# State-space layer of a hybrid backbone: output weights loaded ahead of the last running sums, two state buffers, the variance of y on another engine, one product moved

## What is computed

```python
def step(h, inp):
    xc, ac, Bc, Cc = inp
    acum = jnp.cumsum(ac, axis=1)
    Lm = jnp.exp(jnp.where(tri, acum[:, :, None, :] - acum[:, None, :, :], -jnp.inf))
    CB = jnp.einsum('blgn,bsgn->bgls', Cc, Bc)
    y_diag = jnp.einsum('bgls,blsgr,bsgrp->blgrp', CB, Lm, xg)
    y_off = jnp.einsum('blgn,bgrpn->blgrp', Cc, hg) * jnp.exp(acum)[..., None]
    h_new = jnp.exp(acum[:, -1])[:, :, None, None] * h + jnp.einsum('bsgn,bsgr,bsgrp->bgrpn', Bc, w_end, xg)
    return h_new, y_diag + y_off

def gated_rms_norm(y, z, w):          # groups of 256 columns
    g = y * jax.nn.silu(z)
    return g * lax.rsqrt(jnp.mean(g * g, axis=-1) + EPS) * w
```

## Time and profile before

| | |
|---|---|
| median of 3 executions | 1497.12 us (1496.01 to 1497.76) |
| profiled execution, its own time | 1492.21 us |
| its span, first to last instruction | 1491.0 us |
| PE busy | 1354.5 us (91%) |
| DVE busy | 940.1 us (63%) |
| ACT busy | 773.5 us (52%) |
| POOL busy | 437.3 us (29%) |
| second layer's groups | from about 862 us; the last group's own work 1320 to 1386 us |
| one steady group (groups 1 to 6) to the next | 64.9 us |

### The profile page before, as it was taken

How to read it: one execution, slowest core, us unless ns; L and a number is a source line. 1 busy time by engine, 2 the same in 40 slices (tenths; PEclk the granted TensorE clock), 3 DMA queues, 4 the chain that set the end, 5 groups by cost and what they waited for, 6 DMA issues and landing times.

```text
span 1491.0 us, 22906 instructions
## 1 busy us (share of the span) xinstructions
PE 1354.5 (91%) x8120; PEld 1179.8 (79%) x8120; DVE 940.1 (63%) x1661; ACT 773.5 (52%) x1566; POOL 437.3 (29%) x411
## 2 busy tenths in 40 slices
PE   4999899999999999989997989899999999976797
PEld 4888898899889889868876778887878888765575
DVE  4696656566665666554107668887888888867312
ACT  4432556556555645543217556666666667555331
POOL 0000012112111112113222253544446364435243
PEclk9999999999999999999999999999999999997898
DMA  9344112111112111235412132323222232422531
GB/s 366 110 162 142 43 60 99 56 53 53 62 59 90 53 54 54 74 120 161 147 41 107 43 90 85 98 70 110 87 84 93 76 99 70 112 71 64 211 107 56
DMA packets 46933, 141.31 MB, mean 95 GB/s; under 512 B 5920, under 2 KB 6432, under 8 KB 46880
## 3 DMA queue, kind: packets, MB, share of 16 engines
q1 hardware_dynamic: 42272, 130.12, 26.5%
q10 hardware_dynamic: 4608, 10.49, 2.2%
HBM read 125.78 MB, written 14.81 MB: 94 GB/s over the span
## 4 chain that ended last, share of the span: by engine, by line
PE 48%; DVE 16%; ACT 11%; issue 10%; POOL 8%; DMA 4%; SPq 1%; DVEq 0%; ACTq 0%; POOLq 0%
PE psL L1947 13%; PE psC L1947 6%; PE psS L1932 3%; POOL xw L1909 3%; PE psS L1934 3%; PE psS L1933 3%; ACT X L1016 2%; PE psT L2093 2%; PE psV L1932 2%; PE psV L1934 2%; PE psV L1933 2%; DMA Y1raw<-y_spill 2%; PE psL L1932 2%; PE psL L1934 2%; PE psL L1933 2%
## 5 line engine op out<-in xcount | busy, mean ns | idle before, releaser
L1775 POOL TENSOR_TENSOR wlo<-wraw,whi 128x1024 fp32r<-128x1024 f32 x63 | 150.7, 2393 | 481.9 <-ACT whi L649 402.3
L1947 PE MATMUL psL<-hhi,whi 128*128 128x512 f32 x304 | 123.5, 406 | 0.0
L1947 PE MATMUL psL<-hlo,whi 128*128 128x512 f32 x304 | 122.5, 403 | 0.0
L1947 PE MATMUL psL<-hhi,wlo 128*128 128x512 f32 x304 | 120.6, 397 | 0.0
L2254 PE MATMUL psL<-h1hi,whi 128*128 128x512 f32 x256 | 103.4, 404 | 0.3 <-DVE X L1520 0.3
L2254 PE MATMUL psL<-h1lo,whi 128*128 128x512 f32 x256 | 102.0, 399 | 0.0
L2254 PE MATMUL psL<-h1hi,wlo 128*128 128x512 f32 x256 | 101.9, 398 | 0.0
L1357 DVE TENSOR_REDUCE smax<-psS 128x1 f32<-128x256 f32 (+3 forms) x96 | 67.9, 708 | 51.3 <-PE psS L1934 51.3
L1388 DVE TENSOR_TENSOR PTlo<-psT,PThi 128x256 fp32r<-128x256 f32 (+3 forms) x96 | 68.1, 709 | 48.8 <-ACT PThi L807 47.5
L649 ACT ACTIVATE whi<-wraw 128x1024 fp32r<-128x1024 f32 x54 | 56.6, 1051 | 62.3 <-PE psV L1934 62.3
L1947 PE MATMUL psC<-hhi,whi 128*128 128x256 f32 x280 | 81.9, 292 | 4.9 <-ACT whi L649 2.2
(11 more groups left out here) (423 smaller groups left out, 4486.2 us busy)
## 6 DMA issues: line engine op xcount, KB each, us to landing
wraw<-in_w_ssm SPq DMA_DIRECT2D x48, 512.0 KB, 3.2
wraw<-in_w_in SPq DMA_DIRECT2D x40, 512.0 KB, 3.9
wraw<-in_w_out SPq DMA_DIRECT2D x32, 512.0 KB, 4.1
sums<-sum_spill SPq DMA_DIRECT2D x32, 512.0 KB, 4.8
ada<-in_w_ada SPq DMA_DIRECT2D x16, 512.0 KB, 14.3
wraw<-in_w_ada_late SPq DMA_DIRECT2D x16, 512.0 KB, 4.5
X<-in_xc SPq DMA_DIRECT2D x12, 512.0 KB, 9.6
y_spill<-Yst SPq DMA_DIRECT2D x16, 384.0 KB, 2.5
```

The source lines that it names most:

```text
L1775: G_.tensor_tensor(wlo[:, par], wraw[:, slot], f(whi[:, par]), ALU.subtract).then_inc(s_weight_lo, 1)
L1947: last = PE_.matmul(out, a, b, start=i == 0 and not shared, stop=i == 3 * KT - 1, skip_group_check=True)
```

## The change

1. SP issues the first four loads of output weights before the running sums of chunks 2 and 3 of the last group; before, two came between these and two behind both.
2. `hcur` becomes two buffers. Step i writes buffer i % 2 and reads the other one. DVE's addition in step i waits for the lo part of step i - 2 and not of step i - 1, and only from i = 3.
3. The variance: ACT's square takes a scale, so that its sum is the mean (a quarter of it, as before) at once, and writes its unused squares into `ynm`. POOL adds EPS from a new tile `tiny` ahead of its power. `variance1` on DVE goes, and DVE gets a wait for its own gated tile of the chunk before.
4. PE makes the diagonal product of chunk 0 in state step 4 right behind the state's own product, ahead of two half projections; before it came behind them.

```diff
+    tiny = sbuf(keep, "tiny", [P, 1])
...
-        hcur = sbuf(s, "hcur", [P, DIRS * GW])
+        hcur = sbuf(s, "hcur", [P, 2, DIRS * GW])
...
+        for c in range(NR):
+            out1_load(c)
         sums_load(SSM_GROUPS - 1, 2)
-        for c in range(NR):
-            if c == 2:
-                sums_load(SSM_GROUPS - 1, 3)
-            out1_load(c)
+        sums_load(SSM_GROUPS - 1, 3)
         y1_store(SSM_GROUPS - 1)
...
-            A_.activation(y1[:, 0:GW], yg, ACT.Square, accum_out=yss[:, 0:1]).then_inc(s_y_squares, 1)
+            A_.activation(ynm[:], yg, ACT.Square, scale=(0.25 / GW) ** 0.5, accum_out=yss[:, 0:1]).then_inc(s_y_squares, 1)
...
-                    A_.activation(Hhi[:, i - 1, 0, :], hcur[:, 0:GW], ACT.Copy)
-                    A_.activation(Hhi[:, LT - i, 1, :], hcur[:, GW:2 * GW], ACT.Copy).then_inc(s_state_hi, 1)
+                    A_.activation(Hhi[:, i - 1, 0, :], hcur[:, i % 2, 0:GW], ACT.Copy)
+                    A_.activation(Hhi[:, LT - i, 1, :], hcur[:, i % 2, GW:2 * GW], ACT.Copy).then_inc(s_state_hi, 1)
...
-        def variance1(g, c):
-            dve.wait_ge(s_y_squares, LT * g + c + 1)
-
-            V_.tensor_scalar(yvv[:, 0:1], yss[:, 0:1], 0.25 / GW, EPS, ALU.mult, ALU.add).then_inc(s_y_variance, 1)
-
...
-                    V_.tensor_tensor(by_head(hdec[:], HD), by_head(hcur[:], HD), per_head(GP[:, R_DEC + i], 0, DIRS, HD),
+                    V_.tensor_tensor(by_head(hdec[:], HD), by_head(hcur[:, (i - 1) % 2], HD), per_head(GP[:, R_DEC + i], 0, DIRS, HD),
...
-                    if i > 1:
-                        dve.wait_ge(s_state_lo, LT * g + i - 1)
-                    V_.tensor_tensor(hcur[:], hdec[:], ybank[0], ALU.add).then_inc(s_state_new, 1)
+                    if i > 2:
+                        dve.wait_ge(s_state_lo, LT * g + i - 2)
+                    V_.tensor_tensor(hcur[:, i % 2], hdec[:], ybank[0], ALU.add).then_inc(s_state_new, 1)
...
+                if c:
+                    dve.wait_ge(s_y_gated1, n)
                 dve.wait_ge(s_x_d, n + 1)
                 dve.wait_ge(s_y_chunk, n + 1)
                 V_.tensor_tensor(y2, ybank[1][:, 0:GW], xD[:, c % 2], ALU.add).then_inc(s_y_diag_d, 1)
...
-                variance1(g, c)
...
+        G_.memset(tiny[:], EPS)
...
+                pool.wait_ge(s_y_squares, n + 1)
+                G_.tensor_tensor(yvv[:, 0:1], yss[:, 0:1], tiny[:], ALU.add).then_inc(s_y_variance, 1)
                 pool.wait_ge(s_y_variance, n + 1)
                 inv_sqrt(yrs[:, 0:1], yvv[:, 0:1], 1, s_y_rstd)
...
+            def y_diag(c):
+                n = LT * g + c
+                pe.wait_ge(s_cb_decayed_lo, n + 1)
+                if c:
+                    pe.wait_ge(s_y_diag_d, n)
+                for h in range(GH):
+                    x, m = slice(h * HD, (h + 1) * HD), slice(h * P, (h + 1) * P)
+                    last = mm3(ybank[1][:, h * HD:(h + 1) * HD], Mhi[:, m], Mlo[:, m], xthi[:, c, x],
+                               xtlo[:, c, x], True, True)
+                last.then_inc(s_y_chunk, 1)
...
+                if i == STEPS - 1:
+                    pe.wait_ge(s_tokens_lo, g + 1)
+                    y_diag(0)
                 next_part(i)
                 if last_group and i >= 3:
                     out1_fill(i - 3)
             next_part(STEPS)
-            pe.wait_ge(s_tokens_lo, g + 1)
             for c in range(LT):
                 n = LT * g + c
-                pe.wait_ge(s_cb_decayed_lo, n + 1)
                 if c:
-                    pe.wait_ge(s_y_diag_d, n)
-                for h in range(GH):
-                    x, m = slice(h * HD, (h + 1) * HD), slice(h * P, (h + 1) * P)
-                    last = mm3(ybank[1][:, h * HD:(h + 1) * HD], Mhi[:, m], Mlo[:, m], xthi[:, c, x],
-                               xtlo[:, c, x], True, True)
-                last.then_inc(s_y_chunk, 1)
+                    y_diag(c)
```

More of the change, by code:

```diff
@@ L1665, in ssd @@
                 if i == 0:
-                    V_.tensor_copy(hcur[:], ybank[0]).then_inc(s_state_new, 1)
+                    V_.tensor_copy(hcur[:, 0], ybank[0]).then_inc(s_state_new, 1)
                 else:
-                    if i > 1:
-                        dve.wait_ge(s_state_lo, LT * g + i - 1)
-                    V_.tensor_tensor(hcur[:], hdec[:], ybank[0], ALU.add).then_inc(s_state_new, 1)
+                    if i > 2:
+                        dve.wait_ge(s_state_lo, LT * g + i - 2)
+                    V_.tensor_tensor(hcur[:, i % 2], hdec[:], ybank[0], ALU.add).then_inc(s_state_new, 1)
                 if i + 2 < STEPS:
@@ L1914, in state_lo @@
             pool.wait_ge(s_state_hi, LT * g + i)
-            G_.tensor_tensor(Hlo[:, i - 1, 0, :], hcur[:, 0:GW], f(Hhi[:, i - 1, 0, :]), ALU.subtract)
-            G_.tensor_tensor(Hlo[:, LT - i, 1, :], hcur[:, GW:2 * GW], f(Hhi[:, LT - i, 1, :]),
+            G_.tensor_tensor(Hlo[:, i - 1, 0, :], hcur[:, i % 2, 0:GW], f(Hhi[:, i - 1, 0, :]), ALU.subtract)
+            G_.tensor_tensor(Hlo[:, LT - i, 1, :], hcur[:, i % 2, GW:2 * GW], f(Hhi[:, LT - i, 1, :]),
                              ALU.subtract).then_inc(s_state_lo, 1)
```

## The result

| | median of the executions | ratio to the kernel before |
|---|---|---|
| before | 1496.57 us (1495.57 to 1497.76, 4 executions) | |
| changed | 1474.96 us (1470.81 to 1477.21, 4 executions) | 0.9852, 95% interval [0.9829, 0.9876] |
| changed, measured once more | 1476.32 us (before: 1494.38) | 0.9881 [0.9861, 0.9900] |

The kernel became 21.6 us faster, 18.1 in the second measurement. The profiled execution took 1477.21 us against 1492.21, but the first group's C by B product began 2.7 us later in it (873.63 against 870.89), before any edit acts. From there to the end it is 17.7 us shorter, and that is what the trace can explain.

A forecast was written before the change was run, and what follows sets the result against it. PE, 91% busy, was taken as the bound, plus one late weight transfer in the last group. Gains of 9.25 there, 1.3 in group 0 and -0.45 in seven steady groups made 10.1 us: 1497.1 to 1487.0, range 1479 to 1491.5.

The forecast's parts named there:

- the line of the sum for the seven steady groups: Seven steady groups: 3.85 from two state buffers, 2.4 and 1.0 from the variance move, less 7.7 for POOL: -0.45 us.
- edit 2's 0.55 a group: State product in each group: the last addition no longer waits for POOL, gaining PE 0.55 us; the next wait stays unchanged.
- The cost of POOL's holding in the same line (7.7): Chunk 1: POOL's addition and power end behind DVE's instructions, so PE waits 1.1 us a group, 7.7 in seven.
- Edit 1 (8.7): Last group: ACT's 8.56 us wait before the first weight copy goes, plus 0.1 at `Y1raw`: 8.7 us gained.
- Edit 2 (4.4 + 1.3): State steps: 0.55 us in each of eight groups, 4.4, plus 1.3 once in group 0's state step 2.
- Edit 3 (+2.4 + 1.0 - 7.7): Steady groups: 2.4 us gained at `Mlo` of chunk 3, 1.0 at the gate, 7.7 lost to POOL in chunk 1.
- Edit 4 (0): State step 4: the earlier diagonal product gains nothing and costs 0, at most 0.5 us a group.
- POOL is not held: Rival, chance 0.25: POOL's small operations slip between DVE's, cost falls from 1.1 to 0.1 a group; 17.2 off, 1479.9 us.
- The weights are not the only thing late: Rival, chance 0.17, last group: ACT waits at `Y1raw`, 3 to 4 us of the stall return; 1490 to 1491 us.
- slower: Rival, chance 0.04: POOL's holding reaches PE in every chunk; at 1.1 us in each, 31 us cost, 1510 us.
- no change: Rival, chance 0.04: the edits free only waits that come back at the next semaphore, above all in last-group state steps.
- a group over 0.5 us shorter: Listed sign of being wrong, in the groups' length: it would mean that POOL is not held.

The follow-up runs named there:

- only_weights: The kernel before with only the four loads of output weights moved ahead of the last two loads of running sums: 1485.95 us, 0.9943.
- last_addition_waits: The kernel before with two state buffers only, but the addition of state step 4 still waiting for the step before it: 1492.93 us, 0.9992.
- all_but_first_product: The changed kernel with the diagonal product of chunk 0 again behind the two half projections: 1474.74 us, 0.9879 of the kernel before.
- squares_first: The changed kernel with ACT's chunk 1 squares and copy of transposed chunk 0 ahead of a projection evacuation and weight-tile copy, in looped groups: 1469.78 us, 0.9832.
- no_add: The changed kernel with POOL's addition of EPS left out, so the result is slightly another: 1471.23 us, 0.9831 of the kernel before.
- only_two_states: The kernel before with only the two state buffers added: 1489.45 us, 0.9951.
- all_again: The changed kernel, unaltered, measured once more beside the kernel before: 1476.32 us, 0.9881.
- squares_first_again: The same kernel as squares_first, measured once more: 1466.79 us, 0.9808 of the kernel before.
- squares_first_late: squares_first with the diagonal product of chunk 0 again behind the two half projections: 1467.28 us, 0.9815 of the kernel before.

## Why the prediction was wrong

The step that failed is the line of the sum for the seven steady groups, a loss of 0.45 us, and in it two terms: the gains of edit 3 (2.4 + 1.0), which were sized from the idle time beside the rows and are about half of what the edit gave, and edit 2's 0.55 a group, which assumed that the next wait stays as long. The cost of POOL's holding in the same line (7.7) was right. With group 0 the forecast for these groups was 0.85 us off, and 7.5 us came off. Of the 11.5 us between 10.1 and 21.6, 6.6 are this, 1.0 is the last group, and 3.9 are the part ahead of the second layer that no trace places.

*Edit 1 (8.7)*: right, mechanism and size; 8.5 us [6.3, 10.9] alone. SP issued the weights where I had put them, from 1315.10 on, 8.5 us ahead of the group's C by B product (I had 7.7). The copy of `Y1raw` that waited 0.49 us before waits for nothing in the changed kernel, and all of these copies together wait 25.2 us in ten waits, against 26.3 in eleven before, so the stall that one rival expected there did not come.

*Edit 2 (4.4 + 1.3)*: here the step "the next wait (`Mlo` of chunk 1) stays as long and the 0.55 is kept" failed: it fell by 0.18 in the mean, since the shifted DVE instructions now come ahead of POOL's masks. And from the last state step to the end of the product with the states PE gained 0.66 and not 0.55, as ACT's copy now follows its exponentials at once. Together that is the 0.82 of a steady group. The first group gave 1.8 in all (66.5 us with edit 2 alone against 68.3 in only_weights), where I had 0.55 + 1.3. That the sum fits is luck in part: last_addition_waits divides it into 0.8 and 1.0.

*Edit 3 (+2.4 + 1.0 - 7.7)*: the mechanism was right, two of the sizes were not, and this is the larger part of the miss. The loss was right: from the states' product of chunk 2 to the transposes of chunk 1, 3.02 us became 4.08, 1.06 more against my 1.1. The gain at `Mlo` of chunk 3 I took from the idle time that the row records, 0.34. PE in order of time there, before and after:

```profile
1046.77 0.40 PE L2254 MATMUL psL<-h1hi,wlo 128*128 128x512 f32 x1
1047.49 0.30 PE L1932 MATMUL psS<-xthi,Mhi 128*128 128x64 f32 x1 [0.32 <-DVE Mlo L1634]
```

```profile
1045.24 0.39 PE L2253 MATMUL psL<-h1hi,wlo 128*128 128x512 f32 x1
1045.47 0.19 PE L1931 MATMUL psS<-xthi,Mhi 128*128 128x64 f32 x1
```

These starts lie 0.72 us apart before and 0.23 after: 0.49 gained where the bracket says 0.32, since each matmul is drawn 0.40 long though the next one starts 0.235 after it. The product behind also runs 0.11 shorter (1.36 to 1.25). So this wait was worth 0.60, near twice what I counted. The gate's wait gave about 0.25 after what came back at `wlo` and `hcur`, against 0.16. Together 0.60 + 0.25 + 0.1 in small pieces - 1.06 = -0.1 a group, where I had 0.34 + 0.16 - 1.1 = -0.6; between the lengths of groups, 64.79 and 64.76, there is nothing at all.

*Edit 4 (0)*: right in the mean. I had not thought of the clock.

*The line as a whole.* Over all seven groups, from the first C by B product to the last group's:

| | forecast | measured | from |
|---|---|---|---|
| edit 2 | -5.15 | -6.7 | 449.4 alone, against 456.1 |
| edits 3 and 1 beside it | +4.3 | -0.2 | 449.2 in all_but_first_product |
| clock drops | 0 | -0.55 | -1.41 in before's group 0, +0.86 in after's group 6 |
| sum | -0.85 | -7.5 | |

(456.1 is the kernel before, 457.5, without its drop: the clock was 0.57 from 880 to 884 there, and only_weights, with the same code and no drop, has this group at 68.3 instead of 69.7.)

```profile
880.00:884.00 4.00, 4.00 (x14) 3.31 (x14) 3.20 (x4) 1.08 (x3) 4.00 (x6) 0.57 0.16 44
```

So 4.5 us of the miss are edit 3's gains, 1.5 edit 2's, 0.5 the clock. That group 0 shows so much of it and group 6 a loss comes from where one group is divided from the next: edit 3 shortens the end of a group at the gate, by 1.3, and lengthens the beginning of the next by 1.0 to 1.1. Group 0 has only the one, group 6 only the other. *The last group* gave 10.2 for 9.25. Edits 3 and 4 alone gave 1.6 and 2.2 there, the mean clock rose from 0.84 to 0.87, and two executions of the changed kernel differ by 1.2 in it, so I don't split that microsecond.

The rivals: *POOL is not held* gives 1479.9 us, nearer to the result than my own number, and is wrong as a mechanism: in chunks 0 and 1 of the changed kernel POOL's additions and powers end just behind DVE's instruction on SBUF, and in squares_first and no_add they moved as the holding says. That this rival's number lies nearer is chance. *The weights are not the only thing late*, *slower* and *no change* did not happen. Of what I had listed as showing me wrong, "a group over 0.5 us shorter" came true, but for another reason than the one in its bracket.

The best version found is the changed kernel with the squares of chunk 1 issued early: 1466.8 to 1469.8 us in three measurements with and without edit 4, 1.7 to 1.9% below the kernel before.

## What to carry to other kernels

Price a removed PE wait from the distance between the starts of the matmuls around it, less their usual distance, and not from the idle time beside the row. Where two engines hold each other up over SBUF, a shift of half a microsecond decides who waits: list what the other engine has under way at the new time, for the gain and for the loss, and move the producer (here ACT's squares) rather than the small operation. And read a small change from the repeating groups of the trace before the medians, after looking for drops of the granted clock in either kernel.

## What the runs showed of the hardware

A POOL addition of one element a partition takes 0.19 us free and up to 1.25 held (`arrived` in only_two_states), a power 0.55 free and 0.64 (no_add) to 1.49 us held (before, chunk 3). Held additions end 0.04 to 0.05 us behind DVE's instruction on two SBUF tiles, held powers 0.39 to 0.41; the powers beside a DVE instruction that reads PSUM took 0.54 to 0.55. It works the other way too: DVE's instructions went from 1.23 and 0.68 to 1.49 and 1.11 us, and its copy of two columns from 0.16 to 0.60, when POOL's select had started first. The granted clock can fall to half behind twelve matmuls of 64 columns that follow a wait of 1 us, in one execution and not in the next; that moved the starts of the matmuls behind them from 0.12 to 0.21 us apart, and cost 0.9 to 1.1 us a time in groups 1 to 6 where nothing covered it, and 1.4 to 1.6 in group 0 (before against only_weights, all_again against the changed kernel, squares_first_again against squares_first_late).
